# Attention loops: the older unit's transposes ahead of the newest unit's scores, and their copies ahead of the newest exponential

## The chip, the cores and the metric

The kernel runs on 1 core of one Trainium2 chip. The metric is the device time of one execution in microseconds (us); lower is better. Before the change it was run three times: 3884.61, 3886.86 and 3887.87 us, median 3886.86 us.

## The reference, cut to what matters

The reference is a chain of two transformer blocks, each with two layers, over 512 tokens of width 1024. All data is float32. The first block has, beside its projections and its feed-forward part, grouped attention with 8 query heads of 64 and 2 key heads, over 256 context tokens and 512 latent tokens. The second block has 12 causal heads (6 of width 96, 6 of width 64 with a decay bias) over the 512 tokens. What an attention computes is, per head and per block of 128 queries:

```python
s = jnp.einsum('bkgqd,bkmd->bkgqm', qblk, k).astype(jnp.float32)
p = jax.nn.softmax(s, axis=-1).astype(v.dtype)
return jnp.einsum('bkgqm,bkmd->bkgqd', p, v)
```

In the second block the scores above the diagonal are masked, so the query block at place 0, 1, 2 or 3 of a head sees 128, 256, 384 or 512 keys.

## The kernel before, in words

The program is a list of stages, and each engine has its own hand-written instruction stream through that list; engines wait for each other by counting semaphores only. Most of the time goes into the linear stages (lines 726 to 728: three float32r products for each pair of tiles, with both operands split into a high and a low part). They are not touched.

There are five attention stages. In block 1 they are: context attention of layer 0 (8 heads of 2 query blocks, 256 keys), latent attention of layer 0 (8 heads of 4 query blocks, 768 keys), latent attention of layer 1 (the same). In block 2 they are: one for each layer (12 heads of 4 query blocks, 128 to 512 keys). One head and one query block make a **unit**; `u` counts the units of a stage: 16, 32, 32, 48 and 48.

A unit v goes through these steps, each on one engine:

- **scores(v)**, TensorE: products of query and key tiles into a PSUM slot (lines 1012 and 1013 in block 1, 1027 to 1030 in block 2). There are 2 slots in block 1 and 4 in block 2, so scores(u) waits for exp(u - 2) or exp(u - 4).
- **max(v)**, VectorE: negated row maximum (line 1831).
- **exp(v)**, ScalarE: exponential with the maximum as bias and the row sum as second output (line 1388).
- **reciprocal(v)**, VectorE: of the row sum (line 1837). In VectorE's loop it stands in the next round, behind max(v + 1).
- **norm(v)**, GpSimd: probabilities times the reciprocal (line 1976).
- **turn(v)**, TensorE: transposes of the 128x128 tiles of the probabilities into PSUM (line 1046), in groups of up to four; two PSUM banks (4 and 5) take turns, so a group waits until the group two before it has been copied out. With 768 keys a unit has two groups (4 and 2 tiles), otherwise one.
- **copy(v)**: the transposed groups to SBUF. In block 1 every second group is ScalarE's (line 1396) and the others VectorE's (line 1844); in block 2 all are ScalarE's.
- **values(v)**, TensorE: products with the value tiles (line 1067).

The lag is 2 in block 1 and 3 in block 2. In round u the engines work through their queues in this order, before the change:

- TensorE: scores(u), turn(u - lag), values(u - lag - 2).
- ScalarE: exp(u), copy(u - lag), then on some rounds the output of an older head is taken out of PSUM (line 1215, and line 1185 for its high part), and query and key tiles of the next head are split (line 1185).
- VectorE: max(u), reciprocal(u - 1), copy of its group of u - 2 (block 1), then on some rounds the low parts of the next head's tiles and of an older head's output (line 1528). In the latent attention of layer 1 the keys of the second key head are also split at u = 2.
- GpSimd: norm(v) in order; for the last six heads of block 2 also a cast and, for two of them, three memsets of the next head's rows.

In block 1 the next head is prepared in the round of its query block 1 (block 0 in the context stage), in block 2 in the round of query block 1. Two lines of TensorE's stream say what a turn waits for:

```python
pe.wait_ge(S["p_norm"], st.at("p_norm", v + 1))
...
pe.wait_ge(S[n], st.at(n, copies(st, i - 1, act)))
```

Of the kernel before, what the change touches and what calls it, by code (L numbers as in the profile page):

```python
# [18 lines left out]
ACT = mybir.ActivationFunctionType  # L19
# [81 lines left out]
def build_program(nc, a, out):  # L101
    from contextlib import ExitStack
    ctx = ExitStack()
    with ctx:
# [134 lines left out]
        for l in range(L):  # L239
# [22 lines left out]
            for s in more[::-1]:  # L262
                nq = W[s] // P
                keys = C + T if s == "lat" else C
                U = 8 * nq
# [207 lines left out]
        def on_act(st, i):  # L473

            return i % 2 == 0 if st.first else True
# [5 lines left out]
        def lag(st):  # L481
            return 2 if st.first else 3
# [55 lines left out]
        def pt_dst(st, u, kts):  # L538
            return att_pt(st, u, kts[0] * P, (kts[0] + len(kts)) * P)

        def pt_src(i, kts):
            return bank(4 + i % 2, len(kts) * P)
# [6 lines left out]
        with nc.Block() as block:  # L549
# [168 lines left out]
            def _(pe):  # L718
# [85 lines left out]
                for st in stages:  # L804
# [174 lines left out]
                    elif st.kind == "attention":  # L979
# [53 lines left out]
                        def turn_p(v):  # L1033

                            pe.wait_ge(S["p_norm"], st.at("p_norm", v + 1))
                            p = att_p(st, v, n_keys(st, unit(st, v)[1]))
                            for i, (w, kts) in enumerate(groups):
                                if w != v:
                                    continue
                                if i >= 2:  # L1040

                                    act = on_act(st, i - 2)
                                    n = "pt_act" if act else "pt_dve"
                                    pe.wait_ge(S[n], st.at(n, copies(st, i - 1, act)))
                                for j, kt in enumerate(kts):
                                    mm = nc.tensor.transpose(bank(4 + i % 2)[:, j * P:(j + 1) * P], p[:, kt * P:(kt + 1) * P],  # L1046
                                                             ident)
                                mm.then_inc(S["p_turned"], 1)

                        def values(v):  # L1050
# [17 lines left out]
                                                      att_pt(st, v, kt * P, (kt + 1) * P), start=(kt == 0), stop=(kt == nk - 1))  # L1068
                            mm.then_inc(S["pv_done"], 1)
                        for u in range(U + lag(st) + 2):  # L1070
                            if u < U:
                                scores(u)
                            if 0 <= u - lag(st) < U:
                                turn_p(u - lag(st))
                            if u - lag(st) - 2 >= 0:
                                values(u - lag(st) - 2)
                    elif st.kind == "mixer2":
# [72 lines left out]
            def _(act):  # L1150
# [70 lines left out]
                for st in stages:  # L1221
# [153 lines left out]
                    elif st.kind == "attention":  # L1375
                        use_table(ACT.Exp)
                        U = st.heads * st.nq
                        groups = all_groups(st)
                        for u in range(U + lag(st) + 3):
                            if u < U:  # L1380
                                n = n_keys(st, unit(st, u)[1])
                                act.wait_ge(S["s_max"], st.at("s_max", u + 1))
                                if u > lag(st):

                                    done = sum(v < u - lag(st) for v, _ in groups)
                                    act.wait_ge(S["p_turned"], st.at("p_turned", done))
                                i = u % (lag(st) + 1)
                                nc.scalar.activation(att_p(st, u, n), s_slot(st, u, n), ACT.Exp, bias=nmax[:, i:i + 1],
                                                     accum_out=rsum[:, i:i + 1]).then_inc(S["p_exp"], 1)
                            for i, (v, kts) in enumerate(groups):  # L1390
                                if v == u - lag(st) and on_act(st, i):
                                    act.wait_ge(S["p_turned"], st.at("p_turned", i + 1))
                                    if v >= 3:

                                        act.wait_ge(S["pv_done"], st.at("pv_done", v - 2))
                                    nc.scalar.activation(pt_dst(st, v, kts), pt_src(i, kts), ACT.Copy  # L1396
                                                         ).then_inc(S["pt_act"], 1)
                            v = u - lag(st) - 3
                            if 0 <= v < U - 1 and unit(st, v)[1] == st.nq - 1:
                                take_out(st, unit(st, v)[0])  # L1400
                            if u < U and prepares(st, u):
                                if st.first:
                                    prepare(st.qk, *prepares(st, u))
                                else:
                                    prepare2(st, prepares(st, u))
                        take_out(st, st.heads - 1)
                    elif st.kind == "mixer2":
                        for j in range(3):

                            nc.scalar.activation(zt(5 + j), zt(5 + j), ACT.Copy, scale=HD ** -0.5).then_inc(S["fox_q"], 1)  # L1410
                        for k in range(3):
                            nc.scalar.activation(mla_sq[k], zt(k), ACT.Square).then_inc(S["mla_sq"], 1)
                        for k in range(2):
                            act.wait_ge(S["mla_ms"], st.at("mla_ms", k + 1))
                            root(mla_rs[k], bank(4 + k)).then_inc(S["mla_root"], 1)
                        for j in range(3):
                            act.wait_ge(S["fox_vt"], st.at("fox_vt", j + 1))
                            nc.scalar.activation(zt(11 + j), bank(j % 2), ACT.Copy).then_inc(S["fox_vc"], 1)

                        act.wait_ge(S["fox_a"], st.at("fox_a", 1))  # L1420
                        nc.scalar.activation(fox_t[2], fox_t[1], ACT.Exp).then_inc(S["fox_e"], 1)
                        act.wait_ge(S["fox_e"], st.at("fox_e", 1))
                        nc.scalar.activation(fox_t[3], fox_t[2], ACT.Ln, bias=1.0).then_inc(S["fox_e"], 1)
                        for j in range(2):
                            act.wait_ge(S["pool_t"], st.at("pool_t", j + 1))
                            hi_copy(hh_lat[:, 3 + j, :], pool_tmps[j]).then_inc(S["pool_hi"], 1)
                        for t in range(TT):
                            act.wait_ge(S["mla_v"], st.at("mla_v", t + 1))
                            nc.scalar.activation(v_mla[:, t, :], bank(4 + t % 2, 384), ACT.Copy).then_inc(S["mla_vc"], 1)

                        act.wait_ge(S["pool_lo"], st.at("pool_lo", 2))
                        act.wait_ge(S["fox_c"], st.at("fox_c", 1))
                        for hd in range(MLA_H):
                            act.wait_ge(S["mla_q"], st.at("mla_q", hd + 1))
                            nc.scalar.activation(mla_qt[hd][0:MLA_D, :], bank(hd % 2)[0:MLA_D, :], ACT.Copy,
                                                 scale=1.0 / math.sqrt(MLA_D)).then_inc(S["mla_qc"], 1)
                            act.wait_ge(S["mla_k"], st.at("mla_k", hd + 1))
                            nc.scalar.activation(mla_kt[hd][0:64, :], bank(2 + hd % 2)[0:64, :], ACT.Copy
                                                 ).then_inc(S["mla_kc"], 1)
                            if hd == 0:  # L1440

                                act.wait_ge(S["mla_qf"], st.at("mla_qf", 1))
                            nc.scalar.activation(mla_kt[hd][64:96, :], zt(14)[64:96, :], ACT.Copy).then_inc(S["mla_kc"], 1)
                            if hd == 0:

                                hi_copy(fox_cr[0:FOX_H, :], zt(15)[0:FOX_H, :]).then_inc(S["c_hi"], 1)
                            if hd == 3:
                                act.wait_ge(S["mla_qf"], st.at("mla_qf", 2))
                                act.wait_ge(S["mla_kc"], st.at("mla_kc", 2))
                                prepare2(st, 0)  # L1450
                    elif st.kind == "store":
                        for i in range(2 * TT):
                            act.wait_ge(S["y_turned"], i + 1)
                            nc.scalar.activation(z[:, 4096 + i * 512:4096 + (i + 1) * 512], bank(i % 4), ACT.Copy
                                                 ).then_inc(S["y_copied"], 1)
# [560 lines left out]
```

## Time and profile before

| | |
|---|---|
| median of 3 runs | 3886.86 us |
| profiled execution, its own time | 3885.39 us |
| its span, first to last instruction | 3883.5 us |
| mean granted TensorE clock | 0.954 |
| TensorE matmul busy | 3570.8 us (92%) |
| VectorE busy | 1879.1 us (48%) |
| ScalarE busy | 1199.8 us (31%) |
| GpSimd busy | 361.2 us (9%) |
| in the chain that ended last: TensorE, VectorE, ScalarE | 81%, 9%, 4% |

A profile row of an instruction gives its start in us from the span's start, its duration, engine, line, operation, what is written from what, a count if several are merged, and in brackets how long the engine had been idle before and what ended it. PE is TensorE, DVE VectorE, ACT ScalarE, POOL GpSimd. Ends of matmuls are modelled and overlap the next start, so the distance between starts is the time that they take from the engine. A float32 product of line 1067 stands as two instructions.

### The profile page before, as it was taken

What the parts mean: (1) busy time and instruction counts of PE and PEld (TensorE: products, weight loads), DVE (VectorE), ACT (ScalarE), POOL (GpSimd) and SP (SyncE); (2) the same over time, 40 slices, a digit from 0 to 9 for tenths busy, and PEclk for the clock granted to TensorE, in tenths of its full rate; (3) what the DMA queues carried; (4) which work ended last, traced back from release to release, by engine and by line L of the source; (5) the groups of instructions that cost most, each with busy time, mean ns of one, the idle gap of its engine ahead of it and who ended that gap; (6) DMA issues with size and microseconds to landing.
All of it is one profiled execution on the core that took longest, in us unless ns stands there. A gap on an engine that the chain in (4) does not pass through costs nothing.

```text
span 3883.5 us, 47911 instructions
## 1 busy us (share of the span) xinstructions
PE 3570.8 (92%) x17280; PEld 2933.3 (76%) x17280; DVE 1879.1 (48%) x2754; ACT 1199.8 (31%) x1879; POOL 361.2 (9%) x408
## 2 busy tenths in 40 slices
PE   8937999999996799999999967999999998789998
PEld 4827878888865668888888837888888886478886
DVE  5475575544445544445434454544443453544343
ACT  3125331221222533333223236322232322543232
POOL 1002310000110220001000102100100010120001
PEclk8958999999998899999999978999999999899999
DMA  5300123333311013333333310333323333013332
GB/s 191 104 22 17 57 90 111 111 125 114 97 49 55 1 44 97 94 96 97 101 89 103 87 33 1 89 104 89 103 87 101 94 92 88 1 34 97 95 95 81
DMA packets 535083, 313.94 MB, mean 81 GB/s; under 512 B 14174, under 2 KB 507960, under 8 KB 534968
## 3 DMA queue, kind: packets, MB, share of 16 engines
q1 hardware_dynamic: 534968, 312.43, 26.9%
q8 instruction: 69, 1.13, 0.1%
q14 instruction: 46, 0.38, 0.0%
HBM read 310.30 MB, written 2.10 MB: 80 GB/s over the span
## 4 chain that ended last, share of the span: by engine, by line
PE 81%; DVE 9%; ACT 4%; issue 4%; DMA 1%; POOL 1%; SPq 1%; DVEq 0%; ACTq 0%; POOLq 0%
PE ps L726 24%; PE ps L727 24%; PE ps L728 24%; PE ps L1067 2%; DVE nmax L1831 2%; PE ps L1046 1%; DVE scr L1788 1%; ACT scr L1396 1%; PE ps L787 1%; PE ps L830 1%; DVE scr L1620 1%; DVE hl_lat L1612 1%; PE ps L1124 1%; DMA w_raw<-in_w_out 1%; ACT w_hi_sb L1160 1%
## 5 line engine op out<-in xcount | busy, mean ns | idle before, releaser
L1472 DVE TENSOR_TENSOR w_lo_sb<-w_raw,w_hi_sb 128x1024 fp32r<-128x1024 f32 (+1 forms) x460 | 589.8, 1282 | 1375.5 <-ACT w_hi_sb L1160 1373.9
L1160 ACT ACTIVATE w_hi_sb<-w_raw 128x1024 fp32r<-128x1024 f32 (+1 forms) x460 | 508.1, 1105 | 1460.8 <-PE ps L728 1395.2
L726 PE MATMUL ps<-hh_lat,w_lo_sb 128*128 128x512 f32 x1952 | 772.7, 396 | 39.7 <-DVE hl_lat L1612 22.6
L727 PE MATMUL ps<-hl_lat,w_hi_sb 128*128 128x512 f32 x1952 | 765.3, 392 | 0.0
L728 PE MATMUL ps<-hh_lat,w_hi_sb 128*128 128x512 f32 x1952 | 764.2, 391 | 0.0
L726 PEld LDWEIGHTS ps<-hh_lat,w_lo_sb 128*128 128x128 f32 x1952 | 369.4, 189 | 133.5 <-issue 25.2
L728 PEld LDWEIGHTS ps<-hh_lat,w_hi_sb 128*128 128x128 f32 x1952 | 369.6, 189 | 78.3
L727 PEld LDWEIGHTS ps<-hl_lat,w_hi_sb 128*128 128x128 f32 x1952 | 369.8, 189 | 74.5 <-issue 1.0
L726 PE MATMUL ps<-h2h,w_lo_sb 128*128 128x512 f32 x704 | 275.1, 391 | 1.9 <-DVE z L1720 1.5
L727 PE MATMUL ps<-h2l,w_hi_sb 128*128 128x512 f32 x704 | 273.9, 389 | 0.0
L728 PE MATMUL ps<-h2h,w_hi_sb 128*128 128x512 f32 x704 | 273.9, 389 | 0.0
L726 PE MATMUL ps<-m2h,w_lo_sb 128*128 128x512 f32 x704 | 273.9, 389 | 0.0
L727 PE MATMUL ps<-m2l,w_hi_sb 128*128 128x512 f32 x704 | 273.9, 389 | 0.0
L728 PE MATMUL ps<-m2h,w_hi_sb 128*128 128x512 f32 x704 | 273.9, 389 | 0.0
L726 PE MATMUL ps<-m1h_lat,w_lo_sb 128*128 128x512 f32 x512 | 201.9, 394 | 2.7 <-DVE x_ctx L1665 2.7
L727 PE MATMUL ps<-m1l_lat,w_hi_sb 128*128 128x512 f32 x512 | 200.9, 392 | 0.0
L728 PE MATMUL ps<-m1h_lat,w_hi_sb 128*128 128x512 f32 x512 | 200.7, 392 | 0.0
L1976 POOL TENSOR_SCALAR scr<-scr,rinv 128x768 f32<-128x768 f32 (+2 forms) x128 | 86.1, 672 | 852.0 <-DVE rinv L1837 851.8
L726 PEld LDWEIGHTS ps<-h2h,w_lo_sb 128*128 128x128 f32 x704 | 132.1, 188 | 31.5 <-DVE z L1720 2.3
L1939 POOL TENSOR_TENSOR x_ctx<-x_lat 128x512 f32<-128x512 f32 x7 | 7.3, 1040 | 1586.9 <-DVE x_lat L1665 1586.9
L727 PEld LDWEIGHTS ps<-h2l,w_hi_sb 128*128 128x128 f32 x704 | 132.1, 188 | 27.5 <-issue 0.5
L728 PEld LDWEIGHTS ps<-m2h,w_hi_sb 128*128 128x128 f32 x704 | 132.1, 188 | 27.5
(277 smaller groups left out, 5454.1 us busy)
## 6 DMA issues: line engine op xcount, KB each, us to landing
w_raw<-in_ffn_w_gu SPq DMA_DIRECT2D x176, 512.0 KB, 3.8
w_raw<-in_w_ff SPq DMA_DIRECT2D x128, 512.0 KB, 4.0
w_raw<-in_ffn_w_down SPq DMA_DIRECT2D x64, 704.0 KB, 4.5
z<-in_w_mod SPq DMA_DIRECT2D x64, 512.0 KB, 5.1
w_raw<-in_w_in SPq DMA_DIRECT2D x56, 512.0 KB, 3.8
w_raw<-in_w_out SPq DMA_DIRECT2D x32, 512.0 KB, 4.0
scr<-in_w_mod SPq DMA_DIRECT2D x16, 512.0 KB, 5.2
scr<-in_w_mod SPq DMA_DIRECT2D x3, 2048.0 KB, 12.1
```

The costliest lines, as they stand in the source:

```text
L726: nc.tensor.matmul(dst, wl, hi[:, k, 0:n], start=(k == 0), stop=False)
L727: nc.tensor.matmul(dst, wh, lo[:, k, 0:n], start=False, stop=False)
L728: mm = nc.tensor.matmul(dst, wh, hi[:, k, 0:n], start=False, stop=(k == kt - 1))
L787: mm = nc.tensor.matmul(bank(b)[:, 2 * m + c:2 * m + c + 1], feed_acc(n, c)[:, m * P:(m + 1) * P], one_col[:], start=True, stop=True)
L830: mm = nc.tensor.matmul(bank(5 + n % 3)[0:2, :], silu_c[:, :, k], mod_slot(n % 3)[:, k, :], start=(k == 0), stop=(k == KD - 1))
L1046: mm = nc.tensor.transpose(bank(4 + i % 2)[:, j * P:(j + 1) * P], p[:, kt * P:(kt + 1) * P], ident)
L1067: mm = nc.tensor.matmul(bank(6 + hd % 2)[:, qt * P:(qt + 1) * P], val, att_pt(st, v, kt * P, (kt + 1) * P), start=(kt == 0), stop=(kt == n ...
L1124: mm = nc.tensor.matmul(bank(hd % 2)[0:MLA_D, :], wq_b[:, k, hd * MLA_D:(hd + 1) * MLA_D], zt(k), start=(k == 0), stop=(k == 1))
L1160: nc.scalar.activation(w_hi_sb[:, slot, 0:kt * P], w_raw[:, slot, 0:kt * P], ACT.Copy).then_inc(S["w_hi"], 1)
L1472: nc.vector.tensor_tensor(w_lo_sb[:, slot, 0:kt * P], w_raw[:, slot, 0:kt * P], w_hi_sb[:, slot, 0:kt * P].bitcast(F32), ALU.subtract).the ...
L1831: nc.vector.tensor_reduce(nmax[:, i:i + 1], s_slot(st, u, n), AX.X, ALU.max, negate=True).then_inc(S["s_max"], 1)
L1976: nc.gpsimd.tensor_scalar(pr, pr, rinv[:, i:i + 1], 0.0, ALU.mult, ALU.add).then_inc(S["p_norm"], 1)
```

## The change

In TensorE's loop turn(u - lag) is moved ahead of scores(u). In ScalarE's loop the copies of the groups of unit u - lag are moved ahead of exp(u). VectorE's and GpSimd's streams, the lags, the buffers and the number of instructions stay as they are. All five attention stages use these two loops.

```diff
                         for u in range(U + lag(st) + 2):
+                            if 0 <= u - lag(st) < U:
+                                turn_p(u - lag(st))
                             if u < U:
                                 scores(u)
-                            if 0 <= u - lag(st) < U:
-                                turn_p(u - lag(st))
                             if u - lag(st) - 2 >= 0:
                                 values(u - lag(st) - 2)
...
                         for u in range(U + lag(st) + 3):
+                            for i, (v, kts) in enumerate(groups):
+                                if v == u - lag(st) and on_act(st, i):
+                                    act.wait_ge(S["p_turned"], st.at("p_turned", i + 1))
+                                    if v >= 3:
+
+                                        act.wait_ge(S["pv_done"], st.at("pv_done", v - 2))
+                                    nc.scalar.activation(pt_dst(st, v, kts), pt_src(i, kts), ACT.Copy
+                                                         ).then_inc(S["pt_act"], 1)
                             if u < U:
                                 n = n_keys(st, unit(st, u)[1])
                                 act.wait_ge(S["s_max"], st.at("s_max", u + 1))
...
-                            for i, (v, kts) in enumerate(groups):
-                                if v == u - lag(st) and on_act(st, i):
-                                    act.wait_ge(S["p_turned"], st.at("p_turned", i + 1))
-                                    if v >= 3:
-
-                                        act.wait_ge(S["pv_done"], st.at("pv_done", v - 2))
-                                    nc.scalar.activation(pt_dst(st, v, kts), pt_src(i, kts), ACT.Copy
-                                                         ).then_inc(S["pt_act"], 1)
```

## Rows read from the trace of the kernel before

**Rows 1.** Busy time by stretch: latent attention, layer 0; first attention of block 2. Columns as headed.
```profile
core 0: us, PE busy (x) PEld busy (x) DVE busy (x) ACT busy (x) POOL busy (x), PEclk, DMA share, GB/s
328.80:434.70 105.90, 91.76 (x704) 85.57 (x704) 51.28 (x107) 57.56 (x115) 29.00 (x32) 0.98 0.01 3
...
2317.90:2425.30 107.40, 86.34 (x562) 81.01 (x563) 45.77 (x126) 66.32 (x186) 32.04 (x60) 0.85 0.00 1
```

**Rows 2.** Transposes, line 1046: what ended TensorE's idle time before them (us, times).
```profile
  POOL scr L1976: 73.5, 58
  ACT scr L1396: 51.6, 43
```

**Rows 3.** Timeline of the latent attention, layer 0: one unit in full, and a wait.
```profile
405.04 0.47 PE L1012 MATMUL ps<-k_hi,q_hl 128*128 128x512 f32 x1
...
405.70 0.28 PE L1013 MATMUL ps<-k_lo,q_hl 128*128 128x256 f32 x1
...
405.94 0.85 PE L1046 MATMUL ps<-konst,scr 128*128 128x128 f32 x6
406.01 0.96 DVE L1831 TENSOR_REDUCE nmax<-ps 128x1 f32<-128x768 f32 x1 [1.34 <-PE ps L1013]
406.62 1.50 PE L1067 MATMUL ps<-scr 128*128 128x128 f32 x12
406.89 0.15 DVE L1837 RECIPROCAL rinv<-rsum 128x1 f32<-128x1 f32 x1
...
407.00 0.90 ACT L1388 ACTIVATE scr<-ps,nmax 128x768 f32<-128x768 f32 x1 [0.59 <-DVE nmax L1831]
407.13 0.91 POOL L1976 TENSOR_SCALAR scr<-scr,rinv 128x768 f32<-128x768 f32 x1 [1.78 <-DVE rinv L1837]
...
407.88 0.47 PE L1012 MATMUL ps<-k_hi,q_hl 128*128 128x512 f32 x1
...
409.17 0.69 DVE L1528 TENSOR_TENSOR q_hl<-z,q_hl 64x512 fp32r<-64x512 f32 x1 [1.80 <-ACT q_hl L1185]
...
412.38 0.85 PE L1046 MATMUL ps<-konst,scr 128*128 128x128 f32 x6 [0.87 <-ACT scr L1396]
```

**Rows 4.** Timeline, same stage: exp(1), norm(0), turn(0) at its start; exp(31) near its end.
```profile
331.93 0.89 ACT L1388 ACTIVATE scr<-ps,nmax 128x768 f32<-128x768 f32 x1
...
332.32 0.91 POOL L1976 TENSOR_SCALAR scr<-scr,rinv 128x768 f32<-128x768 f32 x1 [7.70 <-DVE rinv L1837]
...
333.28 0.88 PE L1046 MATMUL ps<-konst,scr 128*128 128x128 f32 x6 [0.23 <-POOL scr L1976]
...
426.22 0.90 ACT L1388 ACTIVATE scr<-ps,nmax 128x768 f32<-128x768 f32 x1 [2.66 <-DVE nmax L1831]
```

**Rows 5.** Timeline of the context attention: a pair of units, maxima and norm.
```profile
311.95 0.42 DVE L1831 TENSOR_REDUCE nmax<-ps 128x1 f32<-128x256 f32 x1
...
312.53 0.48 POOL L1976 TENSOR_SCALAR scr<-scr,rinv 128x256 f32<-128x256 f32 x1 [2.92 <-DVE rinv L1837]
312.68 0.41 DVE L1831 TENSOR_REDUCE nmax<-ps 128x1 f32<-128x256 f32 x1
```

**Rows 6.** Timeline of block 2's first attention: query blocks 1 and 2 of two heads.
```profile
2333.25 0.48 ACT L1396 ACTIVATE scr<-ps 128x384 f32<-128x384 f32 x1
...
2333.62 0.58 ACT L1215 ACTIVATE scr<-ps 64x512 f32<-64x512 f32 x1
...
2335.97 0.55 DVE L1831 TENSOR_REDUCE nmax<-ps 128x1 f32<-128x384 f32 x1
...
2336.68 0.48 POOL L1976 TENSOR_SCALAR scr<-scr,rinv 128x256 f32<-128x256 f32 x1 [3.39 <-DVE rinv L1837]
...
2337.86 0.41 PE L1046 MATMUL ps<-konst,scr 128*128 128x128 f32 x2 [1.03 <-ACT scr L1396]
```

**Rows 7.** TensorE's busy time and granted clock in two neighbouring stretches of the latent attention.
```profile
334.80:338.20 3.40, 1.44 (x11) 1.00 0.00 0
338.20:341.60 3.40, 3.40 (x18) 0.50 0.01 2
```

## The prediction

> **What bounds the kernel now.** I read the page first: TensorE is busy for nine tenths of the span, and nearly all of that is the linear stages, which the change does not touch. So everything is decided in the five attention stages. The view of busy time by stretch gives their length and shows that the latent attention keeps TensorE busy for 91.76 of 105.90 us at a clock of 0.98, and block 2's attention for 86.34 of 107.40 us at 0.85 [rows 1]. The view of what TensorE's transposes wait for names two releasers: ScalarE's copies (51.6 us in 43 waits) and GpSimd's norm (73.5 us in 58 waits) [rows 2]. The timeline then shows how a unit goes through the engines, and which wait ends last in a round [rows 3].
>
> The reader is to see two things there. First, the wait that the change aims at: a turn waits 0.87 us for the ScalarE copy of the unit before, because that copy stands behind an exponential, which stands behind a maximum that VectorE reached late [rows 3]. Second, how little room the norm has. Unit v's reciprocal stands on VectorE behind max(v + 1), so norm(v) starts only 1.15 us after scores(v + 1) ended (405.98 to 407.13) and ends at 408.04. The next scores start at 407.88 and take 0.90, so the turn that needs this norm may start from 408.78: it has 0.7 us to spare, and it has them because the scores stand in front of it [rows 3]. The change takes these scores away from there.
>
> **The change, part by part.** Nothing is added or removed: same instructions, no DMA, nothing moved past SP's or GpSimd's queue. Two orders change, and each unit size gives a term.
>
> *Latent attention, steady state.* The new order closes a loop of one round: scores(u - 1) end, max(u - 1), reciprocal(u - 2), norm(u - 2), turn(u - 2), scores(u) end. From rows 3, with 405.98 as the end of the scores (405.70 + 0.28):
> - scores' end to the start of norm: 1.15; norm 0.91; together 2.06.
> - norm's end to the turn: 333.23 to 333.28, 0.05 [rows 4].
> - turn: 405.94 to 406.62, 0.68. Scores from start to end: 405.04 to 405.98, 0.94 [rows 3].
> - Sum: 2.06 + 0.05 + 0.68 + 0.94 = 3.73 us a unit.
>
> TensorE's own work is 2.84 a unit (405.04 to 407.88 [rows 3]); values(u - 4), 1.26 of it, run inside the norm's wait, and about 0.9 stays idle in every round. Now the mean is (426.22 - 331.93)/30 = 3.14 a unit [rows 4].
>
> *The new order on ScalarE.* copy(u - 2) now waits for turn(u - 2) with exp(u), the take-out of an older head and the next head's split queued behind it, and VectorE waits for those. The turn starts 1.62 before the scores end; its first group of four is through some 0.65 later, and a copy of about 0.6 ends 0.4 before the scores do, while exp(u) cannot start before 1.02 after them (405.98 to 407.00). So this costs nothing in the round; the cover is max(u). The next head's low parts on VectorE began 2.17 after exp began and run 0.69 [rows 3]; a copy of 0.6 is now gone from ahead of them, so they end about 3.3 after the scores, inside 3.73. The wait for ScalarE's copy goes altogether: it is done a whole round early. Late next is norm.
>
> *Latent attention, whole stage.* turn(0) starts at 333.28 as now; scores(2), now behind it, end at 333.28 + 0.68 + 0.94 = 334.90. Twenty-nine rounds of 3.73 bring the scores of unit 31 to 443.07, exp(31) to 444.09, against 426.22: +17.9. Behind it the drain is shorter, since turn(30) no longer waits for a copy and comes ahead: I take -0.9, bounds 0 and -2. So +17 for the stage, and +34 for the two. Bounds: the loop could be 0.15 shorter or longer a round (overlap of modelled ends; scores at 0.90 to 0.94, VectorE late when it also lowers an output), 30 x 2 x 0.15 = 9 us either way.
>
> *Context attention, 256 keys.* Two maxima follow each other by 0.73 now (311.95 to 312.68). In the new order the second needs norm of the unit before: 0.58 to its start, 0.48, 0.05, two transposes at 0.68/6 each (0.23) and short scores of about 0.5, together 1.84 [rows 5]. That is +1.1, less one ScalarE copy (0.37, 2333.25 to 2333.62 [rows 6]) that leaves the chain of take-out and split behind the exponential: +0.75 for each pair of units, seven pairs, +5. Bounds +3 and +10 (TensorE's share doubled at the low clock).
>
> *Block 2.* Its lag of 3 leaves more room. The chain that sets a head is: max of query block 2 (2335.97), then the wait that ends in turn(query block 1) at 2337.86, 1.89 later, then values, the scores of block 1 of the next head, its exponential, copy, take-out, split, low parts, and the next max. In the new order that turn follows its norm (2336.68 + 0.48 + 0.05 = 2337.21): -0.65. The copy leaves the chain: -0.37. But the scores of query block 0 (four products of 128, about 0.45) and a turn of three tiles (0.34) now stand in it [rows 3, 6]. Net -0.23 a head at the high clock, +0.56 at the low one, where the added 0.79 doubles. The stage's clock of 0.85 [rows 1] means the low level for 30% of it: 24 x (0.7 x -0.23 + 0.3 x 0.56) = about 0. Bounds -5 and +13.
>
> **Sum.** 34 + 5 + 0 = +39 us on the profiled execution's 3885.4, so 3924; the median of the runs shown is 1.5 above it: 3926.
>
> **The clock.** In the latent stage the granted clock fell to 0.50, the level of 1.2 GHz, behind a stretch in which TensorE was busy for 1.44 of 3.40 us [rows 7]; the new steady state has it busy for about 2.8 of 3.73, and at the low level it would be busy all the time, from which rows 7 show it returning. So the sum stands at 2.4 GHz. Against that speaks the Trainium skill's page "TensorE: Matmul & The Clock Gate": Part 4 says that transposes do not count as busy time for the clock in the way that other matmuls do, and Part 1 that the throttled state is the default which activity lifts. By that rule the stage would hang at the low level, the second rival; no row here separates transposes from the rest.
>
> **The rivals.**
> - *The norm is in time* and the change gains what it aims at. Then the turns' waits for ScalarE go and no other takes their place: 30 x 2 x (3.14 - 2.84) = 18 in the latent stages, 5 in block 2, so 3864. For it: 51.6 us of such waits [rows 2]. Against it: 0.7 of room against 0.90 of scores taken away. It decides if norm(v) starts more than 0.2 earlier after scores(v + 1) than in rows 3, which VectorE's order does not allow. Chance 0.04.
> - *The clock falls in the latent stages.* TensorE's 2.84 a unit doubles to 5.7, 1.95 above 3.73, over 60 units: +117, so about 4043. Against it the busy share above. Chance 0.03.
> - *The waits only change names.* Norm's wait turns out no longer than the present mean wait (0.30 a unit), because the loop is short by the bound and more, or the drain and block 2 give it back: within 8 us of 3887. It needs a loop of about 3.2, half a microsecond less than any reading of rows 3. Chance 0.03.
>
> **How the numbers follow.** The forecast, slower by about 1%, has 0.90; with the clock rival slower has 0.93, faster 0.04, same 0.03; a measurement of this kernel can tell about 0.2%, 8 us. The range takes the bounds of the terms together, mostly independent: 9 for the latent loop and a few for its drain, 2 and 5 for the context stage, 5 and 13 for block 2; 3905 to 3942. The rivals lie outside it.
>
> **What would show it.** In the profile of the changed kernel: the transposes' idle time put down to GpSimd's norm in nearly every latent unit, about 0.9 each, some 55 us more in total, and next to none to ScalarE's copies; exponentials of the latent stage 3.7 apart and even, where they are now uneven; both latent stages near 123 us long; the context stage near 41; block 2's within a few us of now. The linear stages the same. I am wrong if the exponentials stay near 3.1 apart, if the clock of the latent stretch is well under 0.95, or if the ScalarE copies still end waits.

## The result, and the profile after

The changed kernel takes 3932.1 us (median of 4 runs, 3926.27 to 3933.66) where the kernel before took 3886.23 us in the same comparison: ratio 1.0115, 95% interval 1.0098 to 1.0133. That is 45.9 us more; 39 were forecast, within a range from 3905 to 3942 us. The profiled execution has a span of 3929.2 us.

First the part that answers to [rows 2]: what TensorE's transposes (line 1046) waited for in the changed kernel (us, times).

```profile
  POOL scr L1976: 244.4, 203
  POOL z L1976: 0.4, 2
```

The waits for ScalarE's copy, 51.6 us before, are gone, all 43 of them, and the waits for GpSimd's norm grew from 73.5 to 244.4 us. This view adds up matmuls and weight loads, which are shown as two queues with idle times of their own and wait for the same norm. The groups in the list of lines keep them apart (busy us, mean ns of one, idle before with what ended it). The rows shown here are of the transposes out of `scr`; those of the last six heads of block 2 read `z`, 168 of them, and have no idle time in either kernel. The matmuls of the kernel before:

```profile
L1046 PE MATMUL ps<-konst,scr 128*128 128x128 f32 x488 | 81.8, 290 | 58.7 <-ACT scr L1396 51.6 <-POOL scr L1976 7.1
```

and of the changed kernel, with line 1386, ScalarE's copy in the new numbering, which now waits for transposes:

```profile
L1046 PE MATMUL ps<-konst,scr 128*128 128x128 f32 x488 | 86.2, 300 | 111.6 <-POOL scr L1976 111.5
...
L1386 ACT ACTIVATE scr<-ps 128x512 f32<-128x512 f32 (+3 forms) x168 | 82.9, 493 | 60.1 <-PE ps L1046 58.8
```

Busy time by stretch, answering to [rows 1] and [rows 7]; columns as there. The first three are the two latent stages and block 2's first attention; the last two are parts of the first latent stage.

```profile
337.00:463.20 126.20, 95.67 (x705) 86.62 (x704) 50.87 (x107) 61.28 (x116) 28.98 (x32) 0.96 0.01 4
1304.60:1431.40 126.80, 97.62 (x704) 88.18 (x704) 52.96 (x108) 60.54 (x114) 28.98 (x32) 0.94 0.00 1
2364.00:2468.50 104.50, 83.26 (x561) 77.86 (x562) 45.70 (x126) 69.39 (x186) 32.05 (x60) 0.89 0.00 1
341.00:352.00 11.00, 5.63 (x27) 4.86 (x27) 3.48 (x7) 4.53 (x10) 2.72 (x3) 0.61 0.00 0
355.00:458.00 103.00, 80.21 (x611) 72.85 (x611) 43.21 (x92) 52.95 (x100) 26.01 (x29) 1.00 0.00 1
```

So the matmuls' idle time before transposes is 52.9 us more (58.7 to 111.6), and this is where the time went; before, nearly all of it was ScalarE's copy. A part of it came back: the scores, which now stand behind the turn, had 37.4 us of idle time before them (lines 1012 and 1027) and have 18.9. The latent stage is 20 us longer with the same work in it: VectorE and GpSimd are busy as long as before, ScalarE and TensorE 4 us more each, TensorE from the clock at the stage's start. Block 2's attention is not longer. One steady round of the latent stage, from the timeline (line 1396 is exp, 1386 ScalarE's copy), shows why; it answers to [rows 3].

```profile
363.08 0.87 PE L1046 MATMUL ps<-konst,scr 128*128 128x128 f32 x6 [0.78 <-POOL scr L1976]
363.71 0.47 PE L1012 MATMUL ps<-k_hi,q_hl 128*128 128x512 f32 x1
363.77 0.60 ACT L1386 ACTIVATE scr<-ps 128x512 f32<-128x512 f32 x1 [0.79 <-PE ps L1046]
...
364.49 1.50 PE L1067 MATMUL ps<-scr 128*128 128x128 f32 x12
364.69 0.96 DVE L1831 TENSOR_REDUCE nmax<-ps 128x1 f32<-128x768 f32 x1 [2.34 <-PE ps L1013]
365.56 0.15 DVE L1837 RECIPROCAL rinv<-rsum 128x1 f32<-128x1 f32 x1
...
365.68 0.90 ACT L1396 ACTIVATE scr<-ps,nmax 128x768 f32<-128x768 f32 x1 [1.31 <-DVE nmax L1831]
365.81 0.91 POOL L1976 TENSOR_SCALAR scr<-scr,rinv 128x768 f32<-128x768 f32 x1 [2.78 <-DVE rinv L1837]
...
366.77 0.87 PE L1046 MATMUL ps<-konst,scr 128*128 128x128 f32 x6 [0.78 <-POOL scr L1976]
```

Read it as a circle: turn 363.08, scores 363.71, maximum 364.69, reciprocal 365.56, norm 365.81 to 366.72, next turn 366.77. That is 3.69 us, and every link starts where the one before lets it. The reciprocal and the norm are of the unit before the one whose maximum they follow; they wait for nothing of their own, only for their place behind that maximum. ScalarE's copy ends at 364.37, 1.3 us before exp can start: its new wait costs nothing.

### The profile page after: what moved, and what is told of

Read it like the earlier page. It is cut to its first block, busy times and chain, and to the rows that moved or that the text cites. A ratio compares the mean times of both kernels' runs of the same rounds, so it can differ in the third digit from the quotient of the medians.

```text
span 3929.2 us, 47911 instructions
## 1 busy us (share of the span) xinstructions
PE 3579.1 (91%) x17280; PEld 2935.4 (75%) x17280; DVE 1878.3 (48%) x2754; ACT 1213.4 (31%) x1879; POOL 361.2 (9%) x408
## 4 chain that ended last, share of the span: by engine, by line
PE 82%; DVE 9%; issue 4%; ACT 3%; POOL 2%; DMA 1%; SPq 1%; DVEq 0%; POOLq 0%; ACTq 0%
PE ps L726 24%; PE ps L727 24%; PE ps L728 24%; PE ps L1046 2%; POOL scr L1976 2%; PE ps L1067 1%; DVE nmax L1831 1%; DVE scr L1788 1%; PE ps L787 1%; PE ps L830 1%; DVE scr L1620 1%; PE ps L1012 1%; PE ps L1013 1%; DMA w_raw<-in_w_out 1%; DVE hl_lat L1612 1%
## 5 line engine op out<-in xcount | busy, mean ns | idle before, releaser
L1831 DVE TENSOR_REDUCE nmax<-ps 128x1 f32<-128x768 f32 (+4 forms) x176 | 114.2, 650 | 172.8 <-PE ps L1013 115.1
L1046 PE MATMUL ps<-konst,scr 128*128 128x128 f32 x488 | 86.2, 300 | 111.6 <-POOL scr L1976 111.5
L1046 PEld LDWEIGHTS ps<-konst,scr 128*128 128x128 f32 x488 | 55.8, 148 | 133.0 <-POOL scr L1976 132.9
```

What stands on the lines that cost most here:

```text
L1831: nc.vector.tensor_reduce(nmax[:, i:i + 1], s_slot(st, u, n), AX.X, ALU.max, negate=True).then_inc(S["s_max"], 1)
```

## The experiments

Ten kernels. The table gives, from the starts of the exponentials in each timeline, the us from the first to the last of them in each attention stage (a stage's length without its drain), and the median of the whole.

| kernel | context | latent 0 | latent 1 | block 2, 0 | block 2, 1 | median |
|---|---|---|---|---|---|---|
| before | 29.3 | 95.2 | 96.5 | 96.1 | 93.9 | 3886 |
| changed | 35.7 | 115.4 | 115.9 | 93.1 | 95.6 | 3932 |
| e1 TensorE's half | 39.0 | 128.6 | 131.1 | 110.2 | 109.9 | 3991 |
| e2 ScalarE's half | 31.7 | 86.0 | 88.7 | 89.9 | 88.3 | 3856 |
| e3 changed, reciprocal first | 32.7 | 93.5 | 95.9 | 93.6 | 95.1 | 3881 |
| e4 before, reciprocal first | 31.0 | 97.1 | 97.8 | 101.0 | 100.0 | 3902 |
| e5 changed, norm doubled | 42.8 | 143.6 | 144.6 | 108.2 | 100.7 | 4017 |
| e6 before, norm doubled | 32.1 | 99.5 | 103.1 | 94.6 | 96.8 | 3902 |
| e7 e2, reciprocal early | 27.3 | 82.8 | 86.1 | 79.4 | 79.1 | 3824 |
| e8 changed, reciprocal early | 29.7 | 91.8 | 96.1 | 84.2 | 84.4 | 3857 |
| e9 change in block 2 only | 29.3 | 93.6 | 96.5 | 94.0 | 96.8 | 3884 |
| e10 e7, early in every round of block 1 | 29.0 | 83.4 | 87.4 | 79.2 | 79.6 | 3829 |

### e1 and e2: the two halves apart

The theory: what sets the time in the latent stages is a loop of one round through whatever the turn waits for, closed by TensorE's half of the change. The rival: ScalarE's half costs, because exp now stands behind a copy that waits.

e1 is the kernel before with this:

```diff
+                            if 0 <= u - lag(st) < U:
+                                turn_p(u - lag(st))
                             if u < U:
                                 scores(u)
-                            if 0 <= u - lag(st) < U:
-                                turn_p(u - lag(st))
```

> TensorE's half of the change alone: turn(u - lag) ahead of scores(u), ScalarE's copy again behind exp(u). Theory (the time is set by a loop of one round through whatever a turn waits for): in the latent stages the ScalarE copy now ends 2.52 after the scores (exp at 1.03, 0.89, copy 0.60), later than the norm's 2.12, so a round is 3.69 + 0.54 = 4.2 us and the two stages take about 31 us more than with both halves; block 2 gets its wait for the copy back, up to 24 us more; about 3985 us, and the turns' idle time is put down to ScalarE. Rival (ScalarE's half is what costs, because exp now waits behind a copy that waits for transposes): this kernel is near 3887 us. Second rival (ScalarE's order does not matter either way): 3932 us, exponentials 3.69 apart.

Measured: 3990.9 us (3984.8 to 3992.2), ratio 1.0261, 1.0243 to 1.0278. Behind the first few, the latent exponentials stand 4.20 apart (4.19 to 4.21 but for a 4.38 or 4.39 now and then). Block 2's two stages are 31 us longer than with both halves, where up to 24 were expected. In the timeline of e1's latent stage, line 1396 is the copy in the old place:

```profile
369.52 0.59 ACT L1396 ACTIVATE scr<-ps 128x512 f32<-128x512 f32 x1
370.25 0.84 PE L1046 MATMUL ps<-konst,scr 128*128 128x128 f32 x6 [1.31 <-ACT scr L1396]
```

The turn now waits 1.31 us in every round, for the copy. The loop runs through exp and copy, as worked out.

e2 is the changed kernel with that edit undone:

```diff
-                            if 0 <= u - lag(st) < U:
-                                turn_p(u - lag(st))
                             if u < U:
                                 scores(u)
+                            if 0 <= u - lag(st) < U:
+                                turn_p(u - lag(st))
```

> ScalarE's half of the change alone: copies of u - lag ahead of exp(u), TensorE again scores(u) first. Theory: the scores stand in front of the turn again, the norm has its room, and the turn's wait for the copy is gone, so the latent stages run at TensorE's own 2.84 us a unit (18 us less than before in the two) and block 2 loses up to 1.0 us a head (24 us): 3842 to 3860 us, faster than before. Rival (ScalarE's half costs): exp(u) starts later behind the copy, 3900 us or more. Second rival (the halves only work together): 3887 us.

Measured: 3856.2 us (3855.5 to 3857.3), ratio 0.992, 0.9903 to 0.9936: faster than before. The matmuls of its transposes in the list of lines:

```profile
L1046 PE MATMUL ps<-konst,scr 128*128 128x128 f32 x488 | 81.6, 289 | 32.3 <-POOL scr L1976 31.2
```

The 51.6 us of waits for ScalarE are gone; 24 us of waits for norm have come in part of their place, and 26 us are won there. The two latent stages are 17 us shorter than before, 18 expected, and block 2's 12; the context stage is 2 longer.

The four kernels together: TensorE's half costs 104 us with ScalarE's old order (3991 against 3887) and 76 with the new one (3932 against 3856); ScalarE's half gives 30 us or 59. Taken in the order ScalarE, TensorE, the change is -30 and +76. The rival falls.

### e3 and e4: the reciprocal ahead of the next maximum

If norm(v) is late only because its reciprocal stands behind max(v + 1), then moving the reciprocal opens the loop with the change left in. The edit, made to the changed kernel (e3) and to the one before (e4):

```diff
                         for u in range(U + lag(st) + 3):
+                            if 1 <= u <= U:
+                                ...
+                                nc.vector.reciprocal(rinv[:, i:i + 1], rsum[:, i:i + 1]).then_inc(S["p_inv"], 1)
                             if u < U:
                                 n = n_keys(st, unit(st, u)[1])
...
-                            if 1 <= u <= U:
-                                ...
-                                nc.vector.reciprocal(rinv[:, i:i + 1], rsum[:, i:i + 1]).then_inc(S["p_inv"], 1)
```

> The changed kernel with VectorE's reciprocal(u - 1) moved ahead of max(u); the rest of the change stays. Theory (the loss comes from norm(v) hanging behind max(v + 1), which hangs behind scores(v + 1)): norm(v) now follows exp(v), the loop is open, the latent stages run at about 2.84 us a unit and the time falls from 3932 to 3850 us (3838 to 3870). Rival (the loss is the mere order on TensorE and ScalarE, transposes delaying scores): the time stays at 3932 us, exponentials near 3.7 apart.

> The control for the run before: the kernel before, with reciprocal(u - 1) ahead of max(u) alone. Theory: in the old order the norm was in time in the latent stages, and the turn waits for ScalarE's copy, which this does not move; 3887 us give or take 8 (context stage some us shorter, where the norm did end waits; block 2's maxima a little later). Rival (the reciprocal's place is a cost by itself, whatever the order of turns): 3850 us here too.

Measured: e3 3880.6 us (3875.8 to 3883.3), ratio 0.998, 0.997 to 0.9989; e4 3902.1 us, ratio 1.0039, 1.0025 to 1.0053. e3 is 51 us faster than the changed kernel, a little more than the change had cost, and 42 of the 51 are in the two latent stages (231.3 to 189.4), so the loop is open; but it misses its number by 30 us. e4 misses too, on the slow side: the reciprocal's place gives nothing in the old order, as the theory has it, but costs 11 of its 15 us in block 2, where VectorE used to run several maxima in one go and now waits for an exponential before each (the exponentials' intervals there are 1.49, 1.20 and 1.01 where they were 1.05, 0.82 and 1.65). That this order is what costs the 11 us is read from the timeline and was not tried by itself. Between e4 and e3 stands the same change as between the two kernels, and with the reciprocal ahead in both it gains 21 us (3902 to 3881), 12 of them in block 2, where it cost 46.

A part of e3's 30 us is to be seen in its latent timeline (line 1831 is now the reciprocal, 1836 the maximum):

```profile
373.84 0.69 DVE L1528 TENSOR_TENSOR hl_lat<-scr,hh_lat 128x512 fp32r<-128x512 f32 x1 [2.00 <-ACT hh_lat L1185]
374.45 0.16 DVE L1831 RECIPROCAL rinv<-rsum 128x1 f32<-128x1 f32 x1
...
374.70 0.91 POOL L1976 TENSOR_SCALAR scr<-scr,rinv 128x768 f32<-128x768 f32 x1 [3.67 <-DVE rinv L1831]
...
375.50 0.90 ACT L1396 ACTIVATE scr<-ps,nmax 128x768 f32<-128x768 f32 x1 [1.20 <-DVE nmax L1836]
375.66 0.87 PE L1046 MATMUL ps<-konst,scr 128*128 128x128 f32 x6 [1.12 <-POOL scr L1976]
```

Rounds with no low parts to make are 2.69 to 2.77, TensorE's own pace. In the others the reciprocal is free of the maximum but stands behind line 1528, the low part of an output, which itself waits 2.00 us for ScalarE; then norm is late again and the turn waits 1.12. The expectation had left those rounds out. They account for some 13 us only: 31 intervals of 2.84 in each latent stage would be 176 us, and the table has 189. The rest of the miss is outside the latent stages, as e8 shows.

### e5 and e6: norm made longer

A second pass of the same size ahead of each norm, in the changed kernel (e5) and in the one before (e6):

```diff
+                            link(nc.gpsimd.tensor_scalar(pr, pr, 1.0, 0.0, ALU.mult, ALU.add))
                             nc.gpsimd.tensor_scalar(pr, pr, rinv[:, i:i + 1], 0.0, ALU.mult, ALU.add).then_inc(S["p_norm"], 1)
```

> The changed kernel with a second GpSimd pass of the same size (times 1.0, in place) ahead of every norm, some 0.97 us more for 768 keys. Theory (norm lies in the loop of every latent round): the round grows by the whole 0.97, from 3.69 to about 4.66, 60 rounds, 58 us; context and block 2 add some 15; about 4005 us (3990 to 4025). Rival (the round is set by TensorE's order or by ScalarE, norm only ends last by a little): well under half of that, 3932 to 3955 us.

> The same second pass in the kernel before. Theory: there the norm has some 0.7 us of room in a latent round, so only 0.3 of the 0.97 shows, in the rounds that no other wait covers: 3897 to 3915 us, at most 30 us over 3887, against some 75 in the changed kernel. Rival (norm weighs the same in both orders): 3955 us or more.

Measured: e5 4017.3 us (two runs, 4015.0 and 4019.6), ratio 1.0341, 1.0321 to 1.0362; e6 3902.5 us (3897.5 to 3905.8), ratio 1.0045, 1.003 to 1.0061. The same work costs 85 us in the changed kernel, 57 of them in the two latent stages, and 19 in the one before. e5's latent timeline:

```profile
380.14 0.60 ACT L1386 ACTIVATE scr<-ps 128x512 f32<-128x512 f32 x1 [1.71 <-PE ps L1046]
381.05 0.96 DVE L1831 TENSOR_REDUCE nmax<-ps 128x1 f32<-128x768 f32 x1 [3.26 <-PE ps L1013]
381.93 0.15 DVE L1837 RECIPROCAL rinv<-rsum 128x1 f32<-128x1 f32 x1
382.04 0.90 ACT L1396 ACTIVATE scr<-ps,nmax 128x768 f32<-128x768 f32 x1 [1.31 <-DVE nmax L1831]
382.17 0.83 POOL L1976 TENSOR_SCALAR scr<-scr 128x768 f32<-128x768 f32 x1 [2.78 <-DVE rinv L1837]
383.09 0.91 POOL L1977 TENSOR_SCALAR scr<-scr,rinv 128x768 f32<-128x768 f32 x1
384.05 0.87 PE L1046 MATMUL ps<-konst,scr 128*128 128x128 f32 x6 [1.70 <-POOL scr L1977]
...
385.66 0.96 DVE L1831 TENSOR_REDUCE nmax<-ps 128x1 f32<-128x768 f32 x1 [3.26 <-PE ps L1013]
```

The second pass adds 0.92 (382.17 to 383.09), and the round goes from 3.69 to 4.61 (381.05 to 385.66): the whole of it, round for round. Norm is in the loop, which a profile's wait alone does not prove.

### e7 and e8: the reciprocal in its own round

This puts reciprocal(u) behind exp(u), ahead of the low parts that stood in its way; `lowers` is true in rounds where VectorE makes low parts:

```diff
+        def lowers(st, u):
+            v = u - lag(st) - 3
+            return bool(prepares(st, u)) or 0 <= v < st.heads * st.nq - 1 and unit(st, v)[1] == st.nq - 1 and unit(st, v)[0] % 2 == 1
...
-                            if 1 <= u <= U:
+                            if 1 <= u <= U and not early(st, u - 1):
...
+                            if u < U and early(st, u):
+                                i = u % (lag(st) + 1)
+                                dve.wait_ge(S["p_exp"], st.at("p_exp", u + 1))
+                                nc.vector.reciprocal(rinv[:, i:i + 1], rsum[:, i:i + 1]).then_inc(S["p_inv"], 1)
```

In e7, made from e2, `early` is `lowers(st, u)`; in e8, made from the changed kernel, it is `st.first or lowers(st, u)`.

> ScalarE's half alone, with reciprocal(u) taken in its own round ahead of the low parts in those rounds where VectorE makes low parts for the next head or of an output. Theory (what is left of the turns' waits comes from norms whose reciprocal stands behind those low parts and behind the next maximum): the long latent rounds of 3.9 us shrink, 9 us in all, and block 2's turn behind the low parts no longer waits 1.2 us, some 13 us in all: 3835 us (3826 to 3848). Rival (those rounds are long because of ScalarE's and VectorE's extra work itself): 3856 us.

> The changed kernel with reciprocal(u) in its own round: in block 1 in every round, in block 2 in the rounds with low parts. The run with the reciprocal only moved ahead of the next maximum left it behind the low parts of the round before, where norm still came late. Theory: with both out of its way the loop is open and latent rounds are 2.76 us nearly throughout: 3850 us (3838 to 3864). Rival (the new order of TensorE costs by itself what that run kept): 3881 us.

Measured: e7 3823.9 us (3823.7 to 3828.3), ratio 0.9843, 0.9827 to 0.986; e8 3856.8 us (3854.0 to 3859.7), ratio 0.9931, 0.9914 to 0.9947. e8 has its number, inside the range at its slow side: with the reciprocal out of the way of maximum and low parts, the changed kernel is 75 us faster than it was, and faster than the kernel before. But its latent rounds are not "2.76 us nearly throughout": they are 2.52 to 2.69 without low parts and up to 3.90 with them, 2.96 on average (91.8/31). Of the 24 us that e8 wins over e3, 20 are in block 2, 3 in the context stage and 1 in the latent stages. In block 2 it differs from e3 in two ways, since it also leaves the other rounds' reciprocals behind the maximum, and the two were not told apart. e7 does better than forecast (3835), and faster than its range: over e2 it wins 32 us, 20 of them in block 2, 6 in the latent stages and 4 in the context stage, where 13 and 9 had been expected for the first two. These two kernels differ in the rounds with low parts alone, so the low parts stood in the reciprocal's way above all in block 2. In its first latent stage TensorE has next to no idle time, and the waits of its transposes out of `scr` are all but gone:

```profile
328.00:413.00 85.00, 82.42 (x642) 78.06 (x642) 52.98 (x104) 56.98 (x110) 28.13 (x32) 0.97 0.00 1
```

```profile
L1053 PE MATMUL ps<-konst,scr 128*128 128x128 f32 x488 | 80.8, 287 | 12.1 <-POOL scr L1987 9.8 <-DVE scr L1851 2.0
```

In e8 the same group and that of `z` (line 1851 is VectorE's copy of its transposed group):

```profile
L1053 PE MATMUL ps<-konst,scr 128*128 128x128 f32 x488 | 85.1, 289 | 40.2 <-POOL scr L1987 18.7 <-DVE scr L1851 14.9 <-ACT scr L1393 6.1
L1053 PE MATMUL ps<-konst,z 128*128 128x128 f32 x168 | 29.2, 293 | 16.2 <-POOL z L1987 16.2
```

e7 is the version to keep: it beats both kernels, by 59 us (1.6%) the one before.

### e9 and e10: block 2 alone, and the pair that differs in TensorE's order only

e9 makes both moves depend on the block: `and not st.first` on turn and copy in the new place, `and st.first` in the old one. TensorE's part, as an edit of the changed kernel:

```diff
-                            if 0 <= u - lag(st) < U:
+                            if 0 <= u - lag(st) < U and not st.first:
                                 turn_p(u - lag(st))
                             if u < U:
                                 scores(u)
+                            if 0 <= u - lag(st) < U and st.first:
+                                turn_p(u - lag(st))
```

> The change, both halves, in the two attention stages of block 2 alone; block 1 keeps the old order. The theory has block 2 at nothing in sum (the wait for the copy goes, the scores and a turn enter the chain): 3886 us, give or take 4, so that the whole loss is block 1's. Rival (block 2 carries part of the loss): 3895 us or more; second rival (lag 3 has the room and block 2 gains what ScalarE's half alone gains there, about 12 us): 3874 us.

Measured: 3883.8 us (3880.8 to 3886.2), ratio 0.9997, 0.9987 to 1.0007. Block 2 carries nothing in sum; the whole loss is block 1's. It is a sum of two parts: ScalarE's half alone had shortened block 2's two stages by 12 us (e2), and TensorE's half takes about as much back.

e10 is e7 with e8's `early`, so that e8 and e10 differ in TensorE's order and nothing else.

> As ScalarE's half with the early reciprocal, but in block 1 in every round, as in the changed kernel with it. Theory: that kernel's latent stages run at TensorE's own pace (2.67 us a unit), nothing is left for the reciprocal to give, and the 33 us between 3824 and 3857 us are TensorE's new order alone: 3824 us, give or take 5. Rival (the reciprocal in every round is what makes the other kernel slower, by holding VectorE until exp has ended): 3840 to 3857 us.

Measured: 3829.4 us (3828.0 to 3831.8), ratio 0.9859, 0.9843 to 0.9876, which overlaps e7's interval; it lies at the edge of what was expected (3824, give or take 5), and the rival (3840 to 3857) falls. Against e8's 3856.8, TensorE's new order costs 27 us even with the loop open, where 33 were expected. The latent stages carry 17 of them (91.8 and 96.1 against 83.4 and 87.4) and block 2 another 10. e10's groups:

```profile
L1053 PE MATMUL ps<-konst,scr 128*128 128x128 f32 x488 | 80.7, 285 | 13.3 <-POOL scr L1987 8.1 <-DVE scr L1851 4.9 <-ACT scr L1393 0.4
L1053 PE MATMUL ps<-konst,z 128*128 128x128 f32 x168 | 28.9, 292 | 5.3 <-POOL z L1987 5.3
```

The idle time before the transposes, both groups together, is 56.4 us in e8 against 18.6, put down to norm and to both copies: with the turn ahead of the scores, it asks for each of them earlier. That is 37.8 us, more than the 27 lost, since e10 has idle time elsewhere: 38.0 us before its scores (lines 1019 and 1034) against 20.1 in e8. Which of the three releasers matters most was not tried.

## Why the prediction was right

Point by point, by its own steps:

- **The loop.** Forecast 3.73 us a round; measured 3.69 in the undisturbed rounds, and (115.42 - 14.85)/27 = 3.72 on average over the last 27, since rounds in which VectorE also lowers an output are 3.81 to 3.90. The parts: turn 0.63 (forecast 0.68), turn's end to maximum 0.98 (0.94 and 0.03), maximum to norm 1.12, norm 0.91, norm to turn 0.05. e5 and e6 show that norm is in it, e3 that it is there because of the place of its reciprocal.
- **ScalarE's order costs nothing and the wait for its copy goes.** Right: no such wait is left, and e2 shows what this half is worth alone, 30 us. The prediction put this gain into its rival as 18 us in the latent stages and 5 in block 2; in e2 they are 17 and 12. The rest of that rival was wrong: norm was not in time. Its 2.84 us for TensorE's own work in a unit was read from a long one: the next unit of the same timeline takes 2.69 (407.88 to 410.57), and e7's first latent stage 2.67 on average (82.8/31). The sum did not use it.
- **A latent stage.** Forecast +17; from first to last exponential +20.2 and +19.4 against +17.9, and the drain from exp(31) to the last take-out 8.0 instead of 8.5 us (forecast -0.9). The step that was mis-sized is the start. Scores(2) ended where it was forecast, but the next two intervals were 5.07 and 4.94 us instead of 3.73, at a mean granted clock of 0.61 (341 to 352 in the stretches above). That is the 2.4 us missing:

```profile
345.82 1.54 PE L1046 MATMUL ps<-konst,scr 128*128 128x128 f32 x6 [2.25 <-POOL scr L1976]
...
347.02 0.78 PE L1012 MATMUL ps<-k_hi,q_hl 128*128 128x512 f32 x1
...
348.68 0.96 DVE L1831 TENSOR_REDUCE nmax<-ps 128x1 f32<-128x768 f32 x1 [3.60 <-PE ps L1013]
```

  The turn takes 1.20 there and the scores to their maximum 1.66, against 0.63 and 0.98 in a steady round. The start was put down to steady rounds, and its clock was left out. The prediction argued that at the low level TensorE would be busy all the time; from 343.5 to 353.6, at a granted clock of 0.50, it was busy for 5.73 of 10.1 us, since the first rounds wait for norm as the later ones do and have no products with values yet (these start at 353.38).
- **Context stage.** Forecast +5; measured +6.5 between exponentials, inside its bounds of 3 and 10. The step of a pair was forecast at 1.84 and is 1.83 or 1.84 in three of the last four pairs, 2.40 in the first two.
- **Block 2.** Forecast about 0 for the two together; measured -3.0 and +1.7, and e9 leaves the median where it was. Only the first of the four terms was looked up in the new trace, so that they add up to nothing for the reasons given is not shown. In the changed kernel the maximum of query block 2 starts at 2382.83 and the turn that ended 1.89 us later in [rows 6] starts 1.24 later, at the figure given:

```profile
2382.83 0.55 DVE L1831 TENSOR_REDUCE nmax<-ps 128x1 f32<-128x384 f32 x1
...
2383.54 0.48 POOL L1976 TENSOR_SCALAR scr<-scr,rinv 128x256 f32<-128x256 f32 x1 [3.02 <-DVE rinv L1837]
...
2384.07 0.44 PE L1046 MATMUL ps<-konst,scr 128*128 128x128 f32 x2 [1.17 <-POOL scr L1976]
```

- **The clock.** In the steady part of the latent stage (355 to 458) TensorE is busy for 80.2 of 103.0 us and the granted clock is 1.00: 2.4 GHz throughout. The second rival did not come. The rule from the Trainium skill's page "TensorE: Matmul & The Clock Gate", Part 4, by which transposes count less towards the clock, did not bring it down here, although six of the matmuls of each round are transposes.
- **What is left.** The stages add up to 6.5 + 20.2 + 19.4 - 3.0 + 1.7 = 44.8 us. The first exponential of all stands 2.3 us later in the changed kernel's profile (296.4 against 294.0), ahead of anything that the change touches; over the experiments this start lies between 293.5 and 296.4, so it is scatter. The forecast was 6 us short, by the starts of the latent stages and the context stage for the most part. The range's two ends were not reckoned alike: the lower one is the bounds added up (9, a few, 2 and 5), the upper one is nearer to their root of squares (9, 5 and 13; added up they give 3953). The time lies inside either.

The idle time before the transposes was to grow by some 55 us, put down to norm; over both releasers it grew by 52.9 for the matmuls. Put down to norm alone it grew by 104.4 for the matmuls, and by 170.9 in the view of [rows 2], so that sign holds for the sum and not for the row that it named. What the prediction misread in [rows 2] is the share of the two: of the 73.5 us put down to norm, only 7.1 were idle time of matmuls, so norm was later than a transpose far more seldom than the row seems to say. The sum did not rest on it.

## What to carry to other kernels

Ahead of swapping two steps in one engine's queue, follow each input of the step that moves forward back through the other queues: here a tiny reciprocal stood behind the maximum of a newer unit, so a turn of two rounds ago hung on scores of one round ago, and the lag of two was a lag of one. A long wait in a profile says who came last, not what it would be worth to come sooner; the order change on the engine that was late (ScalarE) gave 30 us, the one on the engine that waited cost 76. Oldest work first was worse on TensorE in every pair tried here: by 104 and 76 us, and by 27 even where the reciprocal stood in its own round. The best of the kernels has the old TensorE order, the new ScalarE order and that reciprocal: 3824 us.

## What the runs showed that was not expected

- The summed view of an instruction's waits counts the weight-load queue beside the matmul queue: 244.4 us in the changed kernel, of which 111.5 are idle time of matmuls.
- A pass of 0.92 us on GpSimd costs 85 us over the kernel or 19, depending on the order of two TensorE steps (e5, e6).
- The start of the changed kernel's first latent stage ran at a mean granted clock of 0.61 for 11 us, with TensorE busy for 5.63 of them; it cost some 2.4 us there. The start of that stage in the kernel before had its low stretch too ([rows 7]); why this one was longer was not tried.
- The reciprocal ahead of the next maximum cost 15 us in the kernel before (e4), 11 of them in block 2, where it broke up runs of maxima. In e7 it was moved only in the rounds that had low parts to make, and there it gave 32 us over e2, 20 of them in block 2.
